# Two products of 256 tokens in place of one of 512, in parts 3 and 4 of the last stage's upward products

## The reference, cut to what matters

```python
def hybrid_layer(x, mod, norm1, norm2, w_in, ..., w_ff1, w_ff2):
    ...
    h2 = rms_norm_2(x, norm2) * (1.0 + scale2) + shift2
    ff = jnp.square(jax.nn.relu(h2 @ w_ff1)) @ w_ff2
    return x + gate2 * ff
```

## Time and profile before

| what | value |
|---|---|
| median of 3 runs | 3098.12 us (3096.55 to 3098.19) |
| profiled execution, first to last instruction (span) | 3093.8 us |
| TensorE matmuls (PE) | 3056.1 us busy, 99%, 14530 instructions |
| TensorE weight loads (PEld) | 2474.3 us busy, 80%, 14530 instructions |
| VectorE (DVE) | 1673.5 us, 54% |
| ScalarE (ACT) | 1109.1 us, 36% |
| GpSimd (POOL) | 680.3 us, 22% |
| mean granted TensorE clock | 0.997 of 2.4 GHz |

### The profile page before, as it was taken

One profiled execution on the slowest core, in us unless ns is written; L12 is line 12 of the kernel. 1 busy time (PEld: TensorE's weight loads), 2 busy tenths in 40 slices (PEclk: granted clock), 3 DMA queues, 4 the chain that ended last, 5 costly groups with the idle time before them and its releaser, 6 DMA issues.

```text
span 3093.8 us, 36733 instructions
## 1 busy us (share of the span) xinstructions
PE 3056.1 (99%) x14530; PEld 2474.3 (80%) x14530; DVE 1673.5 (54%) x2491; ACT 1109.1 (36%) x1757; POOL 680.3 (22%) x525
## 2 busy tenths in 40 slices
PE   9999999999999999999999999999999999999999
PEld 7888887788888888887788888776788877778887
DVE  6454557554555445536864555677533356763332
ACT  4222344332223332244443222456422333643331
POOL 2101134111011110054211101356211123722110
PEclk9999999999999999999999999999999999999999
DMA  5343422243443334432043444301333331033332
GB/s 190 116 153 126 134 85 72 85 140 116 153 132 126 127 119 153 129 108 62 31 136 119 131 138 134 109 31 53 105 96 96 97 105 62 17 108 102 96 95 75
DMA packets 115802, 329.70 MB, mean 107 GB/s; under 512 B 13616, under 2 KB 19120, under 8 KB 115248
## 3 DMA queue, kind: packets, MB, share of 16 engines
q1 hardware_dynamic: 115632, 327.36, 33.1%
HBM read 325.21 MB, written 2.10 MB: 106 GB/s over the span
## 4 chain that ended last, share of the span: by engine, by line
PE 92%; DVE 4%; ACT 2%; POOL 1%; issue 1%; DMA 0%; DVEq 0%; SPq 0%; ACTq 0%; POOLq 0%
PE ps L70 90%; PE ps L73 1%; ACT s_tmp L76 1%; POOL s_tmp L87 1%; DVE s_tmp L79 1%; DVE s_wl L79 1%; DVE s_tmp L99 0%; ACT s_wh L76 0%; DVE s_small L93 0%; ACT s_hh L76 0%; DVE s_x L82 0%; DVE s_tmpr L79 0%; POOL s_tmp L79 0%; DVE s_hl L79 0%; ACT s_tmpr L76 0%
## 5 line engine op out<-in xcount | busy, mean ns | idle before, releaser
L76 ACT ACTIVATE s_wh<-s_raw 128x1024 fp32r<-128x1024 f32 (+3 forms) x560 | 541.8, 970 | 1109.3 <-PE ps L70 1107.2
L70 PE MATMUL ps<-s_hh,s_wh 128*128 128x512 f32 x2304 | 894.6, 393 | 18.8 <-ACT s_hh L76 11.9
L79 DVE TENSOR_TENSOR s_wl<-s_raw,s_wh 128x1024 fp32r<-128x1024 f32 (+3 forms) x529 | 607.8, 1150 | 532.6 <-ACT s_wh L76 532.3
L70 PE MATMUL ps<-s_hh,s_wl 128*128 128x512 f32 x2304 | 887.7, 390 | 0.2
L70 PE MATMUL ps<-s_hl,s_wh 128*128 128x512 f32 x2304 | 886.9, 390 | 0.3 <-DVE s_hl L79 0.3
L79 POOL TENSOR_TENSOR s_tmp<-s_tmp 128x512 f32<-128x512 f32 (+2 forms) x228 | 315.8, 1389 | 1616.5 <-ACT s_tmp L76 1453.3
L70 PEld LDWEIGHTS ps<-s_hh,s_wh 128*128 128x128 f32 x2304 | 433.3, 188 | 116.0 <-issue 17.1
L70 PEld LDWEIGHTS ps<-s_hh,s_wl 128*128 128x128 f32 x2304 | 433.6, 188 | 93.0 <-DVE s_wl L79 2.9
L70 PEld LDWEIGHTS ps<-s_hl,s_wh 128*128 128x128 f32 x2304 | 433.7, 188 | 92.2 <-issue 2.2
L70 PE MATMUL ps<-s_a0h,s_wh 128*128 128x512 f32 x960 | 377.3, 393 | 0.0
L70 PE MATMUL ps<-s_a0h,s_wl 128*128 128x512 f32 x960 | 373.8, 389 | 0.0
(11 more groups left out here) (141 smaller groups left out, 2995.7 us busy)
## 6 DMA issues: line engine op xcount, KB each, us to landing
s_raw<-in_ff_dram SPq DMA_DIRECT2D x128, 512.0 KB, 3.6
s_tmp<-in_w_mod_dram SPq DMA_DIRECT2D x192, 256.0 KB, 3.5
s_raw<-in_f1i_dram SPq DMA_DIRECT2D x88, 512.0 KB, 3.6
s_raw<-in_f2i_dram SPq DMA_DIRECT2D x88, 512.0 KB, 3.6
s_raw<-in_f1o_dram SPq DMA_DIRECT2D x32, 512.0 KB, 3.5
s_raw<-in_f2o_dram SPq DMA_DIRECT2D x32, 512.0 KB, 3.4
s_raw<-in_hyb_dram SPq DMA_DIRECT2D x28, 512.0 KB, 3.5
s_raw<-in_nsa_dram SPq DMA_DIRECT2D x28, 512.0 KB, 3.6
```

Source lines behind the costliest of these rows:

```text
L70: return self.eng.matmul(o, w, m, **kw) if self.eng is not None else Blank()
L76: return self.eng.activation(o, a, f, **kw) if self.eng is not None else Blank()
L79: return self.eng.tensor_tensor(o, a, b, f) if self.eng is not None else Blank()
```

## The change

In the last stage, for `p >= 2`, each upward unit is computed by two calls of `product` that each take 256 of the 512 tokens (`HALVES`), both into the same bank, each into its own half of it. All 24 terms of the first half are issued before the 24 of the second. The signal that the unit is done goes with the last matmul of the second call. `product` takes the columns as a new argument, whose default is all 512. Everything else is as before: 16 of the stage's 64 units are touched.

```diff
-            def product(b, u, mov, ks, start, stop, at=0):
+            def product(b, u, mov, ks, start, stop, at=0, cols=slice(0, T)):
 
-                c = u % RING
+                c, o = u % RING, ps[:, b, cols]
                 for n, k in enumerate(ks):
                     mh, ml, sig_h, key_h, sig_l, key_l = mov(k)
                     w = slice((k - at) * 128, (k - at + 1) * 128)
                     pe.wait_ge(*w_hi[u])
                     pe.wait_ge(*sig_h[key_h])
-                    pe.matmul(B(b), wh[:, c, w], mh, start=start and n == 0, stop=False)
+                    pe.matmul(o, wh[:, c, w], mh[:, cols], start=start and n == 0, stop=False)
                     pe.wait_ge(*sig_l[key_l])
-                    pe.matmul(B(b), wh[:, c, w], ml, start=False, stop=False)
+                    pe.matmul(o, wh[:, c, w], ml[:, cols], start=False, stop=False)
                     pe.wait_ge(*lo_of(u))
-                    m = pe.matmul(B(b), wl[:, c, w], mh, start=False, stop=stop and n == len(ks) - 1)
+                    m = pe.matmul(o, wl[:, c, w], mh[:, cols], start=False, stop=stop and n == len(ks) - 1)
                 return m
...
                         claim(b)
-                        product(b, u, h_of(s), range(KT), True, True).then_inc(*unit.up(u))
+                        if s == REL_1 and p >= 2:
+                            product(b, u, h_of(s), range(KT), True, True, cols=HALVES[0])
+                            product(b, u, h_of(s), range(KT), True, True, cols=HALVES[1]).then_inc(*unit.up(u))
+                        else:
+                            product(b, u, h_of(s), range(KT), True, True).then_inc(*unit.up(u))
                         free[b] = [(sq_up, (s, p, t))]
```

## The result

The changed kernel takes 3101.06 us in the median of 20 runs (3098.58 to 3105.47); the kernel before, run beside it 20 times, takes 3096.74 us (3094.68 to 3099.18). The ratio is 1.0016 with a 95% interval of 1.0010 to 1.0022: about +5.0 us, from +3.1 to +6.8 us (the two medians differ by 4.3 us). It is a little slower, by 0.16%, which is under the 0.2% that the prediction counts as no change, though the interval reaches 0.22%. 3101.06 us lies in the range of 3096.3 to 3104.8 us. The increase is not the +1.3 us of the forecast, it is the +5.1 us of rival A.

A forecast was written before the change was run, and what follows sets the result against it. TensorE's matmuls were taken to bound the last stage; 768 x 0.115 = 88.3 us added less 87.0 us removed, other terms zero, gave +1.3 us: 3098.1 + 1.3 = 3099.4 us, range 3096.3 to 3104.8 us.

The forecast's parts named there:

- rival A: Touched upward matmuls: step is 13.3 ns fixed plus columns at 2.4 GHz, 120 ns, +5.1 us, 3103.2 us; chance 0.29.
- What bounds the kernel, and that it passes one to one into the end: Last stage: TensorE alone for 330.49 us, so time added in the 16 units goes one to one into the end.
- 384 removed, 768 added, nothing merged: 16 upward units: 384 matmuls of 512 columns (87.0 us) become 768 of 256 with 768 weight loads.
- The value of s: Distance between starts of 256-column matmuls in the touched units: 115 ns, 88.3 us for 768, +1.3 us.
- The floor of loads at 108 to 111 ns: Touched units: weight loads cannot follow faster, so s is not under 108 ns, at lowest -3.7 us.
- rival C: Touched units: weight load starts only after the stream before it, 295 ns a step, +139 us, 3238 us; chance 0.01.
- Instructions cost nothing: 768 more instructions to fetch among 36733: zero cost if the fetches stay ahead.
- rival B: Upward parts 2 and 3: TensorE short of instructions, +6.2 us or more, +15.9 us at 134 ns a pair; chance 0.13.
- Waits, bank, ring: Touched units: no new wait, bank read after the second half as before, weights ready three units ahead; cost zero.
- Rival D: Touched units: loads' 111 ns the only floor, surplus over 213.3 ns belongs to long streams; -1.8 us, 3096.3 us; chance 0.10.

The follow-up runs named there:

- experiment 1: Against the changed kernel, its 16 units cut into 384 and 128 tokens in place of twice 256; 3121.64 us in one run.
- experiment 2: Against the changed kernel, its 16 units computed in four products of 128 tokens each; 3179.48 us in one run.
- experiment 3: Against the changed kernel, both halves of a term issued one after the other, same weights loaded twice; 3101.56 us, ratio 1.0017 to the kernel before.
- bfloat16 kernel: Against the changed kernel, the 16 units' 256-column matmuls take bfloat16 operands from one small tile, their products left out; 3093.28 us in one run.

## Why the prediction was right, and where it was not

The range held because it took in rival A up to 122 ns a step; the value taken, 115 ns, was not what came. The time of 3101.06 us stands only 1.7 us over the 3099.4 us of the forecast, and this nearness is partly luck: the kernel before took 3096.74 us beside it, not the 3098.12 us from which the forecast set out. The change in time was forecast as +1.3 us and is +5.1 us.

*What bounds the kernel, and that it passes one to one into the end:* right. The touched parts grew by 2.6 us each (43.5 to 46.1) and the piece of the chain by their sum.

*384 removed, 768 added, nothing merged:* right, 14914 against 14530 loads and matmuls.

*The value of s:* this is the term that was mis-sized, 115 ns for a measured 120.0. 768 x 0.120 - 87.0 = +5.1 us is what came (the chain grew by 5.12 us). The error was a correction. The rows of the 64-row pairs said 0.12 us a step, and the prediction took 6% or 13 ns off, because the pairs need 0.24 us for 512 columns where the whole array needs 0.227. The surplus is there at 512 columns, but it does not carry over to 256: the pairs' 0.12 us is what the whole array takes too, 120.0 ns. This also answers the prediction's case against rival A. And the prediction then argued from proportion, half of 226.7 ns, where rival A's decomposition into 213.3 + 13.3 ns was the one that experiment 1 confirms at a third width. The reason given for 115 ns, that two streams so near each other seldom mesh without loss, is not what the runs show: the steps are an even 120 ns, and at 384 columns, far from the loads' floor, the same 13.3 ns are paid.

*The floor of loads at 108 to 111 ns:* right at its upper value, 111.5 ns a step in experiment 2, over 1536 matmuls; the 0.1085 us came from the loads of transposes. The loads hide fully beside 256 columns: rival C with its 295 ns is out.

*Instructions cost nothing:* right. The price of rival B (134 ns a pair, from the densest long stretch) was not that of the supply: that stretch mixes many shapes, among them 30 of the kernel's full matmuls of 512 columns, which take 227 ns each by themselves, and experiment 2 runs at 112 ns a pair for 85.6 us. The Trainium skill, "TensorE: Matmul & The Clock Gate", section "Wait — 56ns, not 53.3ns?", gives 62 ns for a matmul in the sequencer with hardware decoding off. In experiment 2 a load and a matmul together take 112 ns for 85.6 us, so two such prices are not paid here.

*Waits, bank, ring:* right. ScalarE's wait for TensorE grew from 18.1 to 20.3 us in a part, that is, its slack grew, and the order of the terms makes no difference (experiment 3).

*Rival D* would have needed the surplus over 213.3 ns to belong to long streams only. It does not with `fp32r` operands; the bfloat16 kernel, which has no such surplus, steps by 109.3 ns. The Trainium skill, "TensorE: Matmul & The Clock Gate", section "Back-to-back issue gap", has 2.5 ns over the columns for a warm matmul; the runs agree with it for bfloat16 (109.3 and 216 ns) and not for `fp32r` (120.0 and 226.7 ns). The prediction noted this at 512 columns (the 226.7 ns are those of the earlier trace rows; the earlier trace rows show the step only as 0.22 us), and gave the conclusion, that the surplus is paid per matmul, only as rival A with a chance of 0.29.

## What to carry to other kernels

When a product is cut into shorter ones, price each piece as its columns at the array's rate plus what a whole one costs beyond its columns, and take half of a whole only where that remainder has been seen to shrink; here 13.3 ns stayed per `fp32r` matmul with a full load of weights, and only 2.6 ns with bfloat16 operands. A weight load recorded longer than the step does not bound the step: look at how close loads follow one another where they are dense (111.5 ns for a recorded 192). In a stage bound by TensorE alone, a cut that brings no one else forward is pure cost (5.1 us here), and repeating it over more units (here 60 in place of 16) lifts a small effect over the noise.

## What the runs showed of the hardware

- `fp32r` matmuls on the whole array with loads of 128 columns step by 120.0, 173.3 and 226.7 ns at 256, 384 and 512 columns, and by 111.5 ns at 128, where the loads are the floor; bfloat16 ones step by 109.3 and 216 ns at 256 and 512.
- A weight load of 128 columns recorded with 192 ns starts every 111.5 ns (experiment 2), and its matmul starts before its recorded end.
- Using fewer than 128 columns of `fp32r` weights (96, 64 and 32 were tried) makes the step longer at 512 moving columns (230.0 to 231.7 ns against 226.7) and shorter at 256 (113.4 to 117.8 against 120.0), least at 64 columns of weights. The cause is open.
- TensorE took an instruction every 56 ns over 85.6 us without running short.
- The stage before the last one ends at another time from execution to execution (the piece above begins at 2742.38 to 2747.80 us in programs that are the same up to there), so two spans are compared here by the piece, not by their ends.
